# Even and odd layers of a three-layer transformer kernel: a moved transpose, two late weight parts, earlier query copies, and scalings shared with GpSimd

## The chip, the cores and the metric

The kernel runs on one core of a Trainium2 chip. A core has five engines that each run a program of their own: TensorE (PE in the profile; its weight loads are shown apart as PEld), VectorE (DVE), ScalarE (ACT), GpSimd (POOL) and SyncE (SP), which here only issues DMAs. The engines meet in semaphores: one instruction raises a semaphore when it ends, and another engine's program stands until the semaphore has the value it waits for. The metric is the device time of one execution in microseconds. The kernel before takes 1057.89 us, the median of three runs (1057.48 to 1059.09).

## What is computed

The program is a whole small model on 256 rows of 1024 columns: a first layer (attention, a recurrent block and a mixture of 32 experts), then two layers of another make, an even one and an odd one, each with a feed-forward block behind it, and a last norm. The change touches only the two later layers. Cut to what matters:

```python
# even layer: one product makes all inputs of two mixers
h = rmsnorm(x, norm_mix)
y = h @ ev_w_in        # qa_nope, qa_rope, c_kv, ka_rope, iq, ik, iw, qb, kb, vb
# dsa_mixer: attention over a latent
c_kv = rmsnorm(c_kv, kv_gain)              # "the latent rows", 128 columns
k_rope = rope(k_rope)
rel = relu(einsum(rope(iq), rope(ik)))     # picks keys for every query
idx = top_k(einsum(rel, iw), T // 4)
s = einsum([q_nope @ w_uk, rope(q_rope)], [c_kv, k_rope][idx])
o_a = (softmax(s) @ c_kv[idx]) @ w_uv
# diff_mixer: two softmaxes, one subtracted from the other
p = softmax(einsum(rope(qb), rope(kb)))    # 4 heads x 2 maps
o_b = rmsnorm((p[0] - lam * p[1]) @ vb)
x = x + concat(o_a, o_b) @ ev_w_out
x = x + swiglu(rmsnorm(x))

# odd layer: three attentions under one gate, 16 heads in 4 groups
y = rmsnorm(x) @ od_w_in   # qc, kc_raw, vc_raw, ks, vs, kw, vw, gates
g = sigmoid(gates)
o_cmp = softmax(rope(q) @ compress(rope(kc_raw))) @ compress(vc_raw)
o_slc = softmax(rope(q) @ rope(ks)[selected blocks]) @ vs
o_win = softmax(rope(q) @ rope(kw)[window]) @ vw
x = x + (g0 * o_cmp + g1 * o_slc + g2 * o_win) @ od_w_out
x = x + swiglu(rmsnorm(x))
```

With 256 rows the selected blocks and the window hold every earlier key, so both parts are plain causal attention, each over its own keys.

## The kernel before

**Products in two parts.** A product `h @ W` is made of f16 numbers: each factor is split into a high part (f16 of the number) and a low part (what is left), and three products are summed, high by high, low by high, high by low. ScalarE makes a weight tile's high part (`high_part`, L290), VectorE its low part (`low_part`, L297). The class `Projection` does this tile by tile over the columns of `W`, in two slots. `multiply` (L383) is one tile on TensorE: 48 matmuls, 16 for each of the three terms, and the weights' low part is only wanted from the 33rd on. Its argument `between` is called after each matmul and can put other work into the middle of a tile. `move` (L395) brings the result from PSUM to `y` on ScalarE. The next load into a slot waits for the low part of the tile before it there.

**Output weights.** The class `OutWeights` does the same for `ev_w_out` and `od_w_out`, in eight parts of 128 rows: `high_part` (L525) on ScalarE, `low_part` (L530) on VectorE, the semaphore `out.low` counting the latter.

**Even input product, `even_in`.** Twelve tiles (k = 0 to 11). Between the tiles stands the side work that needs columns already made. After tile 1 TensorE turns four blocks of `uk` and then the two blocks of the normalized latent rows (`turn`, L3256, waiting for `ckv_normed`); tile 2 follows; then the keys' product, which waits for ScalarE's copy of the turned latent rows (`ckv_out`, L3127). VectorE splits tiles and does one part of the rotary embedding (rope); GpSimd does another (L1487, L1488). Just before the end of tile 11 the keys are turned, which waits for both (`kb_begun`, `kb_ended`).

**Even attention, `even_attention`.** Eight units, four of `diff_mixer` (u = 0 to 3) and four of `dsa_mixer` (4 to 7). A unit is 2 x 256 rows of scores; because of causality each half is done in two row tiles, `SPAN`: tile 0 has 128 rows by 128 keys, tile 1 has 128 rows by 256 keys. TensorE scores a unit, VectorE finds the row minimum (the scores are negated), ScalarE takes exponentials and sums (L3367), VectorE weighs the unit (`weigh`: reciprocal of the sums, L3438, then scalings, L3442), TensorE turns it (L3534), VectorE and ScalarE copy it from PSUM (VectorE's is `left`, L3449), TensorE multiplies by the values (L3555), and ScalarE and VectorE split the result (`rest`, L3453). VectorE's loop runs ahead: in its step u it finds the minimum of unit u + 2, weighs unit u + 1 and copies unit u. The last two low parts of the output weights stand in this loop, after `left(4)` and `left(5)` (`LATE_LOWS`); TensorE waits for all eight (`out.low`) before its first projection, in unit 7.

**Odd input product, `odd_in`.** Ten tiles in the order of `ODD_TILES`. After tile 8 TensorE turns the doubled first keys (L3795), which waits for ScalarE's four copies of the turned queries (L3688, `q_out`) and its doubling of the keys (`keys_twice`); after tile 9 the second keys. At the start of step k ScalarE makes the high part of tile k + 1. VectorE's step k makes the low part of tile k + 1, a rope, and in step 5 the copies of the compressed keys (`c_out`).

**Odd attention, `sparse_attention`.** Sixteen units, two (selected blocks, window) for each of eight pairs of heads. A unit goes the same way as in the even attention. `weigh` multiplies the sums by the gate, takes the reciprocal (L3947) and scales four blocks (L3951). `turn` (L4036) makes six transposes of 128x128, three for each of the two heads: one of tile 0 and two of tile 1.

GpSimd has no part in the odd attention. Each engine's order is written by hand, as the order of these calls in its function.

## Time and profile before

| | before |
|---|---|
| median of three runs | 1057.89 us (1057.48 to 1059.09) |
| profiled execution, its own time | 1059.21 us |
| span of its records | 1057.2 us, 20482 instructions |
| mean granted clock of TensorE | 0.976 of full speed |
| TensorE busy | 967.5 us, 92% |
| VectorE busy | 592.9 us, 56% |
| ScalarE busy | 479.6 us, 45% |
| GpSimd busy | 103.3 us, 10% |
| chain that ended last | TensorE 65%, DMA 13%, VectorE 7%, ScalarE 4% |

The profile is one execution of the program. A row of the timeline has the start in us from the beginning of the span, the duration, the engine, the line of the kernel, the operation, output `<-` input, shapes and count; in brackets stands how long the engine was idle just before, and what ended that. A count above 1 means that several like instructions that follow each other are shown as one row, whose duration runs over all of them. A row of the table of stretches has for each engine the time that it was busy within the stretch, the granted clock of TensorE as a share of full speed, the share of the DMA engines' time and the rate in GB/s. "later_pB" is the PSUM of the later layers, and "field" the large SBUF area in which most of their buffers lie.

The even input product lies at about 425 to 497 us of the span, the even attention to 530, the feed-forward block behind it to 737, the odd input product to 797, the odd attention to 850.

### The profile page before, as it was taken

To read this page: it belongs to the slowest core of one execution; us is meant where nothing else is said; L and a number is where in the kernel's file an instruction comes from. 1 tells how busy PE (TensorE), PEld (TensorE's weight loads), DVE (VectorE), ACT (ScalarE), POOL (GpSimd) and SP (SyncE) were. 2 spreads that over 40 slices of the span, in tenths; PEclk is the share of its full clock that TensorE was granted. 3 is DMA by queue.
4 is the path that set the end of the run, shared out by engine and by line. 5 is a ranking of instruction groups with operands and counts; after the bars stand their busy time and mean duration, and the time that the engine had idled before them with its cause. 6 is when DMAs were issued, how large, how long until landed. Compare 5 with 4: busy or idle time off the path is not lost.

```text
span 1057.2 us, 20482 instructions
## 1 busy us (share of the span) xinstructions
PE 967.5 (92%) x8706; PEld 694.5 (66%) x8706; DVE 592.9 (56%) x965; ACT 479.6 (45%) x822; POOL 103.3 (10%) x110
## 2 busy tenths in 40 slices
PE   6999999989666678999999999999999999999996
PEld 5676896654333344887658777786986558777774
DVE  5577888611000004799766555554888856644643
ACT  5567653410000005665664535436656755553442
POOL 5620550000000001014010000000030000000000
PEclk9999999999888899999999999999999999999998
DMA  9755119899999997765044665673725023757621
GB/s 259 231 156 176 42 42 386 332 411 420 421 421 421 421 414 238 258 219 182 19 165 159 201 220 172 203 234 125 240 88 160 2 103 132 244 179 238 210 69 40
DMA packets 108747, 228.68 MB, mean 216 GB/s; under 512 B 7305, under 2 KB 86203, under 8 KB 94075
## 3 DMA queue, kind: packets, MB, share of 16 engines
q1 hardware_dynamic: 105691, 219.38, 57.7%
q0 software_dynamic: 2976, 8.14, 2.6%
q8 instruction: 60, 0.98, 0.4%
q14 instruction: 20, 0.16, 0.0%
HBM read 224.63 MB, written 1.05 MB: 213 GB/s over the span
## 4 chain that ended last, share of the span: by engine, by line
PE 65%; DMA 13%; DVE 7%; ACT 4%; SPq 2%; issue 2%; DVEq 0%; ACTq 0%
PE later_pB L923 20%; PE later_pB L932 10%; PE later_pB L383 6%; PE later_pB L879 4%; DMA ring<-in_w_down 4%; PE rw_pB L1403 3%; DMA ring<-in_w_up 3%; DMA mix<-in_w_gate 3%; DMA ring<-in_w_gate 3%; PE later_pB L911 2%; SPq L1271 2%; PE rw_pB L2474 1%; PE rw_pB L1424 1%; PE rw_pB L1432 1%; PE later_pB L4036 1%
## 5 line engine op out<-in xcount | busy, mean ns | idle before, releaser
L923 PE MATMUL later_pB<-field 128*128 128x256 f16 x1920 | 212.9, 273 | 0.0
L923 PEld LDWEIGHTS later_pB<-field 128*128 128x128 f16 x1920 | 187.8, 98 | 25.5
L752 DVE SCALAR_TENSOR_TENSOR field<-field 128x2048 f16<-128x2048 f32 x84 | 153.8, 1869 | 57.1 <-ACT field L647 57.1
L647 ACT ACTIVATE field<-field 128x2048 f16<-128x2048 f32 x84 | 126.4, 1567 | 15.8 <-DMA field<-in_ffn_w_up 9.6
L932 PE MATMUL later_pB<-field 128*128 128x512 f16 x528 | 117.7, 379 | 0.6 <-DVE field L752 0.6
L383 PE MATMUL later_pB<-field 128*128 128x256 f16 (+2 forms) x960 | 114.7, 274 | 0.6
L383 PEld LDWEIGHTS later_pB<-field 128*128 128x128 f16 x960 | 94.2, 99 | 13.5 <-ACT field L319 1.8
L1403 PE MATMUL rw_pB<-ring,kept 128*32 128x256 f32 x864 | 69.0, 415 | 25.7 <-DMA ring<-in_w_up 22.7
L932 PEld LDWEIGHTS later_pB<-field 128*128 128x128 f16 x528 | 51.5, 98 | 58.9 <-issue 1.5
L1335 DVE TENSOR_TENSOR rw_mu_a<-rw_pB,rw_mu_a 128x256 f32<-128x256 f32 x8 | 3.4, 424 | 122.9 <-PE rw_pB L1403 122.9
L1403 PEld LDWEIGHTS rw_pB<-ring,kept 128*32 128x32 f32 x864 | 37.9, 120 | 50.6 <-issue 37.1
L768 DVE SCALAR_TENSOR_TENSOR field<-later_pB,field 128x512 f32<-128x512 f32 x22 | 15.2, 691 | 91.6 <-ACT field L665 91.6
L665 ACT ACTIVATE field<-later_pB 128x512 f32<-128x512 f32 x22 | 13.1, 597 | 102.6 <-PE later_pB L923 102.5
L297 DVE SCALAR_TENSOR_TENSOR field<-wt,field 128x2048 f16<-128x2048 f32 (+2 forms) x22 | 52.7, 2397 | 12.2 <-ACT field L290 11.7
L290 ACT ACTIVATE field<-wt 128x2048 f16<-128x2048 f32 (+2 forms) x22 | 42.1, 1916 | 7.9 <-DMA wt<-in_od_w_in 4.3
L1424 PE MATMUL rw_pB<-ring,rw_mu_a 128*32 128x512 f32 x216 | 34.1, 668 | 11.3 <-DMA ring<-in_w_down 7.1
L879 PE MATMUL later_pB<-field 128*128 128x512 f16 x192 | 43.3, 380 | 0.0
L1294 ACT ACTIVATE rw_mu_a<-rw_pB 128x256 f32<-128x256 f32 x8 | 3.1, 388 | 77.9 <-PE rw_pB L1461 77.9
L1432 PE MATMUL rw_pB<-rw_few_y,rw_mu_a 128*128 128x512 f32 x64 | 29.8, 606 | 7.4 <-ACT rw_few_y L1303 6.5
L383 PE MATMUL in_pY<-ring 128*128 128x256 f16 (+1 forms) x288 | 33.8, 269 | 2.4 <-DVE ring L297 1.9
L665 ACT ACT_TABLE_LOAD x8 | 10.3, 1283 | 56.0 <-PE later_pB L923 44.6
L879 PEld LDWEIGHTS later_pB<-field 128*128 128x128 f16 x192 | 18.5, 98 | 21.9 <-issue 1.1
(589 smaller groups left out, 1563.6 us busy)
## 6 DMA issues: line engine op xcount, KB each, us to landing
ring<-in_w_up SPq DMA_DIRECT2D x27, 1024.0 KB, 26.7
ring<-in_w_gate SPq DMA_DIRECT2D x27, 1024.0 KB, 26.4
ring<-in_w_down SPq DMA_DIRECT2D x24, 1024.0 KB, 26.1
field<-in_ffn_w_down SPq DMA_DIRECT2D x22, 1024.0 KB, 5.0
field<-in_ffn_w_gate SPq DMA_DIRECT2D x20, 1024.0 KB, 7.5
field<-in_ffn_w_up SPq DMA_DIRECT2D x20, 1024.0 KB, 9.8
wt<-in_ev_w_in SPq DMA_DIRECT2D x9, 1024.0 KB, 5.8
wt<-in_od_w_in SPq DMA_DIRECT2D x9, 1024.0 KB, 5.5
```

The source lines that it names most:

```text
L290: self.nc.scalar.activation(self.w_hi[:, k % 2, :, 0:n], self.wt[:, k % 2, :, 0:n], ACT.Copy, scale=W_SCALE).then_inc(self.hi_ready, 1)
L297: self.nc.vector.scalar_tensor_tensor(self.w_lo[:, k % 2, :, 0:n], self.wt[:, k % 2, :, 0:n], W_SCALE, self.w_hi[:, k % 2, :, 0:n], ALU.mu ...
L383: ins = self.nc.tensor.matmul(self.pY[:, slot, t, 0:n], x[:, c, t * P:(t + 1) * P], w[:, slot, c, 0:n], start=(term == 0 and c == 0), stop ...
L647: copy = lambda o, i, scale=1.0: nc.scalar.activation(o, i, ACT.Copy, scale=scale)
L665: nc.scalar.activation(gated[:, s, :], pG[:, s, :], ACT.Silu, scale=1.0 / W_SCALE).then_inc(silu_done, 1)
L752: return nc.vector.scalar_tensor_tensor(out, whole, scale, hi, ALU.mult, ALU.subtract)
L879: return nc.tensor.matmul(pY[:, t, half_of(n)], source[:, c, t * P:(t + 1) * P], by[:, c, half_of(n)], start=(c == 0 and term == 0), stop= ...
L923: ins = T.matmul(p[:, s, j * SEQ:(j + 1) * SEQ], w[:, s, m, c, j::NJ], h[:, c, :], start=(n == 0), stop=(n == 3 * KC - 1))
L932: return T.matmul(pY[:, t, half_of(half)], h[:, s, at:at + P], w[:, s, j, half_of(half)], start=False, stop=stop, skip_group_check=True)
L1403: ins = nc.tensor.matmul(into[i * CAP:(i + 1) * CAP, 0:D_EXPERT], h[:, c, i * CAP:(i + 1) * CAP], held[:, c * D_EXPERT:(c + 1) * D_EXPERT] ...
L1424: ins = nc.tensor.matmul(pD[i * CAP:(i + 1) * CAP, half, :], hidT[:, j, i * CAP:(i + 1) * CAP], held[:, at:at + 512], start=(j == 0), stop ...
L1432: ins = nc.tensor.matmul(pY[:, t, half, :], into_tokens[:, g, t * P:(t + 1) * P], y[:, half * 512:(half + 1) * 512], start=(g == 0), stop= ...
```

## The change

Four edits, independent of each other.

**The latent turn.** `even_in` on TensorE: the wait for `ckv_normed` and the two transposes of the latent rows go from behind tile 1's side work into tile 2, after its first 14 matmuls (`between` is called from the ninth on, and `turn_latent` acts at its count 5).

```diff
+        def turn_latent(done):
+            if done == 5:
+                pe.wait_ge(ckv_normed, 1)
+                turn(half(0, 0), lambda t: ckv[:, t, :]).then_inc(ckv_turned, 1)
...
-            pr.multiply(pe, k, turn_keys if k == n_tiles - 1 else None)
+            pr.multiply(pe, k, {2: turn_latent, n_tiles - 1: turn_keys}.get(k))
             if k == 1:
                 pe.wait_ge(rows_in, 5 * 16)
                 pe.wait_ge(pr.low_T, KC)
                 for n in range(4):
                     nc.tensor.transpose(sc[:, 1, n * P:(n + 1) * P], uk[:, n, :], ident)
-                pe.wait_ge(ckv_normed, 1)
-                turn(half(0, 0), lambda t: ckv[:, t, :]).then_inc(ckv_turned, 1)
```

TensorE's order around tile 2 of the even input product, before; the row with two transposes of L3256 is the latent turn, the 96 matmuls are tiles 0 and 1:

```order
L363 MATMUL later_pB<-con_identity,mix 128x128 x16
L383 MATMUL later_pB<-field 128x248 x96
L3276 MATMUL later_pB<-con_identity,field 128x128 x4
L3256 MATMUL later_pB<-con_identity,field 128x128 x2
L383 MATMUL later_pB<-field 128x248 x48
L3282 MATMUL later_pB<-field 128x256 x4
L383 MATMUL later_pB<-field 128x256 x48
```

And after:

```order
L363 MATMUL later_pB<-con_identity,mix 128x128 x16
L383 MATMUL later_pB<-field 128x248 x96
L3281 MATMUL later_pB<-con_identity,field 128x128 x4
L383 MATMUL later_pB<-field 128x248 x14
L3256 MATMUL later_pB<-con_identity,field 128x128 x2
L383 MATMUL later_pB<-field 128x248 x34
L3285 MATMUL later_pB<-field 128x256 x4
```

The two transposes moved behind 14 of tile 2's 48 matmuls; nothing else on TensorE moved there.

**Late low parts.** `even_attention` on VectorE: the low parts 6 and 7 of the output weights leave steps 4 and 5 of the unit loop and come after the loop, ahead of `rest(6)`. On TensorE the wait for all eight parts becomes a wait in each projection, for 6 parts in the first six and for 7 and 8 in the last two.

```diff
-EVEN_LOWS, LATE_LOWS = {1: (0, 1), 2: (2,), 3: (3,), 4: (4,), 5: (5,)}, {4: 6, 5: 7}
+EVEN_LOWS, LATE_LOWS = {1: (0, 1), 2: (2,), 3: (3,), 4: (4,), 5: (5,)}, (6, 7)
...
-            if u in LATE_LOWS:
-                out.low_part(dve, LATE_LOWS[u])
...
             if u >= 6:
                 rest(u - 2)
+        for c in LATE_LOWS:
+            out.low_part(dve, c)
         rest(units - 2)
...
         def project(c):
             pe.wait_ge(low_out, min(c, units // 2) + 1)
+            pe.wait_ge(out.low, max(c + 1, LATE_LOWS[0]))
             project_first(c)
...
             if u == 7:
-                pe.wait_ge(out.low, KC)
                 project(0)
```

VectorE's order in steps 4 and 5 of the even attention before, from `left(4)` on; L530 is a low part of the output weights, L3438 the reciprocal at the head of a weighing:

```order
L3449 COPY field<-later_pB 128x384
L530 SCALAR_TENSOR_TENSOR field<-field 128x1024
L3438 RECIPROCAL ea_part<-ea_den 128x4
L3442 TENSOR_SCALAR field<-field,ea_part 128x128
L3442 TENSOR_SCALAR field<-field,ea_part 128x256
L3442 TENSOR_SCALAR field<-field,ea_part 128x128
L3442 TENSOR_SCALAR field<-field,ea_part 128x256
L3422 TENSOR_REDUCE ea_low_max<-later_pB 128x2 x2
L3449 COPY field<-later_pB 128x384
L530 SCALAR_TENSOR_TENSOR field<-field 128x1024
L3438 RECIPROCAL ea_part<-ea_den 128x4
```

VectorE's order at the end of the even attention after the change, from the last unit's copy on (L3456 is `rest`, L3493 the scaled outputs):

```order
L3456 TENSOR_TENSOR field<-later_pB,field 128x256
L3452 COPY field<-later_pB 128x384
L3456 TENSOR_TENSOR field<-later_pB,field 128x256
L530 SCALAR_TENSOR_TENSOR field<-field 128x1024 x2
L3456 TENSOR_TENSOR field<-later_pB,field 128x256
L3493 SCALAR_TENSOR_TENSOR field<-field,later_pB 128x1024
L3456 TENSOR_TENSOR field<-later_pB,field 128x256
```

Both low parts left the two steps, where a copy is now followed at once by the next reciprocal, and stand together ahead of the third remainder from the end.

**Query copies first.** `odd_in` on ScalarE: the high part of the last tile (9) goes from the start of step 8 to behind the query copies and the doubled keys. On VectorE the copies of the compressed keys go from step 5 to step 6, behind the low part of tile 7 and ahead of the rope of step 6.

```diff
-            if 1 <= k < n_tiles - 1:
+            if 1 <= k < n_tiles - 2:
                 pr.high_part(act, k + 1)
...
                 ins.then_inc(q_out, 1)
-            if k == 8:
                 act.wait_ge(x_turned, 1)
                 act.wait_ge(ks_roped, 1)
                 double(0, 1536).then_inc(keys_twice, 1)
+                pr.high_part(act, 9)
...
-            if 3 <= k <= 6:
-                dve.wait_ge(pr.moved, k)
-                rope(link, nc.vector, part(256 * (k - 3)), r64, tmp)
-            if k == 5:
+            if k == 6:
                 dve.wait_ge(seconds, 1)
                 dve.wait_ge(glink, 3)
...
                 nc.vector.tensor_tensor(o.vc[:], each, own, ALU.mult).then_inc(c_out, 1)
+            if 3 <= k <= 6:
+                dve.wait_ge(pr.moved, k)
+                rope(link, nc.vector, part(256 * (k - 3)), r64, tmp)
```

ScalarE's order in steps 8 and 9 of the odd input product before; L395 moves a tile's result, L290 is the last tile's high part, L3688 the copies of the queries (x4) and the doubled keys (x2):

```order
L395 ACTIVATE field<-later_pB 128x2x256
L290 ACTIVATE field<-wt 128x2432
L3688 ACTIVATE field<-later_pB 128x512 x4
L3688 ACTIVATE field<-field 128x512 x2
L395 ACTIVATE field<-later_pB 128x2x256
L3688 ACTIVATE field<-field 128x512 x2
```

And after:

```order
L395 ACTIVATE field<-later_pB 128x2x256
L3691 ACTIVATE field<-later_pB 128x512 x4
L3691 ACTIVATE field<-field 128x512 x2
L290 ACTIVATE field<-wt 128x2432
L395 ACTIVATE field<-later_pB 128x2x256
L3691 ACTIVATE field<-field 128x512 x2
```

The high part moved behind six copies; the count of instructions is the same.

**GpSimd scales tile 0.** `sparse_attention` gets a program for GpSimd: for every unit it waits for VectorE's reciprocal (`inverted`), scales the two blocks of tile 0 (2 x 128x128, L3942 of the new kernel), and raises `weighed_first`. VectorE scales only the two blocks of tile 1 (2 x 128x256); before it writes the factors of unit u it waits until GpSimd is done with unit u - 2. TensorE turns the four blocks of tile 1 first, then waits for `weighed_first` and turns the two of tile 0.

```diff
+    def gpsimd(pool):
+        t, c0, nk = SPAN[0]
+        wait_alone(pool, begun, cleared, 3)
+        for u in range(units):
+            at = u % 2
+            pool.wait_ge(inverted, u + 1)
+            for i in range(2):
+                into = E[:, at, i, c0:c0 + nk]
+                ins = nc.gpsimd.tensor_scalar(into, into, part[:, at, i, t:t + 1], None, ALU.mult)
+            ins.then_inc(weighed_first, 1)
...
+            if u >= 2:
+                dve.wait_ge(weighed_first, u - 1)
             link(nc.vector.tensor_tensor(part[:, at], den[:, at], gate[:, b + 1, 2 * n:2 * n + 2, :],
                                          ALU.mult))
-            link(nc.vector.reciprocal(part[:, at], part[:, at]))
+            nc.vector.reciprocal(part[:, at], part[:, at]).then_inc(inverted, 1)
+            dve.wait_ge(inverted, u + 1)
+            t, c0, nk = SPAN[1]
             for i in range(2):
-                for t, c0, nk in SPAN:
-                    into = E[:, at, i, c0:c0 + nk]
-                    ins = nc.vector.tensor_scalar(into, into, part[:, at, i, t:t + 1], None, ALU.mult)
+                into = E[:, at, i, c0:c0 + nk]
+                ins = nc.vector.tensor_scalar(into, into, part[:, at, i, t:t + 1], None, ALU.mult)
             ins.then_inc(weighed, 1)
...
-            for i in range(2):
-                for k, (t, kb, at) in enumerate(blocks):
+            for k, (t, kb, at) in sorted(enumerate(blocks), key=lambda b: -b[1][0]):
+                if t == 0:
+                    pe.wait_ge(weighed_first, u + 1)
+                for i in range(2):
                     ins = nc.tensor.transpose(pT[:, i, k * P:(k + 1) * P], E[:, u % 2, i, at:at + P], ident)
```

VectorE's order for one unit of the odd attention before; L3937 is a row minimum, L3945 and L3947 make the factors, L3951 scales, the copy is `left`:

```order
L3937 TENSOR_REDUCE nsa_low_max<-later_pB 128x2 x2
L3945 TENSOR_TENSOR nsa_part<-nsa_den,field 128x4
L3947 RECIPROCAL nsa_part<-nsa_part 128x4
L3951 TENSOR_SCALAR field<-field,nsa_part 128x128
L3951 TENSOR_SCALAR field<-field,nsa_part 128x256
L3951 TENSOR_SCALAR field<-field,nsa_part 128x128
L3951 TENSOR_SCALAR field<-field,nsa_part 128x256
L3958 COPY field<-later_pB 128x384
```

And after:

```order
L3953 TENSOR_REDUCE nsa_low_max<-later_pB 128x2 x2
L3963 TENSOR_TENSOR nsa_part<-nsa_den,field 128x4
L3965 RECIPROCAL nsa_part<-nsa_part 128x4
L3970 TENSOR_SCALAR field<-field,nsa_part 128x256 x2
L3977 COPY field<-later_pB 128x384
```

Of four scalings two are left on VectorE, and 32 scalings of 128x128 (16 units, two each) stand on GpSimd, which had none there.

## Rows read from the trace of the kernel before

**Rows 1.** table of stretches, the odd attention

```profile
797.00:850.00 53.00, 47.82 (x410) 31.27 (x409) 47.45 (x153) 37.20 (x152) 0.00 (x0) 1.00 0.20 64
```

**Rows 2.** timeline of the even input product, around the latent rows

```profile
429.98 0.44 PE L3256 MATMUL later_pB<-con_identity,field 128*128 128x128 f32 x2 [1.12 <-DVE field L3217]
...
430.25 5.24 PE L383 MATMUL later_pB<-field 128*128 128x248 f16 x48
...
433.83 0.59 ACT L3127 ACTIVATE field<-later_pB 128x512 f32<-128x512 f32 x1
```

**Rows 3.** timeline of the even attention, units 3 to 7

```profile
516.11 1.22 DVE L530 SCALAR_TENSOR_TENSOR field<-field 128x1024 f16<-128x1024 f32 x1
...
516.25 0.22 ACT L3367 ACTIVATION_READ_ACCUMULATOR field<-later_pB,ea_low_max 128x1 f32 x1
...
517.24 0.17 DVE L3438 RECIPROCAL ea_part<-ea_den 128x4 f32<-128x4 f32 x1
...
519.95 0.85 PE L3534 MATMUL later_pB<-con_identity,field 128*128 128x128 f32 x6 [1.32 <-DVE field L3449]
...
521.17 0.18 DVE L3438 RECIPROCAL ea_part<-ea_den 128x4 f32<-128x4 f32 x1 [0.19 <-ACT field L3367]
...
522.51 1.55 PE L3555 MATMUL later_pB<-field 128*64 128x256 f32 x8
...
527.76 0.87 PE L3555 MATMUL later_pB<-field 128*64 128x256 f32 x8
...
529.09 0.42 DVE L3453 TENSOR_TENSOR field<-later_pB,field 128x256 f16<-128x256 f32 x1 [2.30 <-ACT field L3387]
```

**Rows 4.** timeline of the odd input product, last two tiles

```profile
781.01 5.40 PE L383 MATMUL later_pB<-field 128*128 128x256 f16 x48
...
782.24 2.23 ACT L290 ACTIVATE field<-wt 128x2432 f16<-128x2432 f32 x1 [2.17 <-DMA wt<-in_od_w_in]
...
784.38 2.04 ACT L3688 ACTIVATE field<-later_pB 128x512 f32<-128x512 f32 x4
...
787.60 1.06 PE L3795 MATMUL later_pB<-con_identity,field 128*128 128x128 f32 x8 [1.18 <-ACT field L3688]
...
788.50 6.36 PE L383 MATMUL later_pB<-field 128*128 128x304 f16 x48
...
791.87 1.15 ACT L3688 ACTIVATE field<-field 128x512 f32<-128x512 f32 x2 [3.92 <-POOLq L3685]
```

**Rows 5.** timeline of the odd attention, turn of one unit on TensorE

```profile
826.18 0.85 PE L4036 MATMUL later_pB<-con_identity,field 128*128 128x128 f32 x6 [0.47 <-issue]
```

**Rows 6.** timeline of the even input product, tile splits and ropes on GpSimd

```profile
449.83 2.28 DVE L297 SCALAR_TENSOR_TENSOR field<-wt,field 128x2048 f16<-128x2048 f32 x1
...
471.75 1.32 POOL L1488 TENSOR_TENSOR field<-field,con_rope 128x512 f32<-128x512 f32 x1
...
472.16 3.07 DVE L297 SCALAR_TENSOR_TENSOR field<-wt,field 128x2048 f16<-128x2048 f32 x1 [0.20 <-ACT field L290]
...
485.07 0.73 POOL L1487 TENSOR_TENSOR field<-field,con_rope 128x256 f32<-128x256 f32 x1 [2.71 <-DVEq L3245]
```

**Rows 7.** timeline: scalings of one odd unit, and the nearest GpSimd instructions

```profile
22.14 2.80 POOL L1671 TENSOR_SCALAR fi_base<-ring 1x1024 f16<-1x1024 f32 x1 [6.49 <-DMA ring<-in_w_uq]
...
63.18 0.67 POOL L1684 CAST low<-con_diagonal 128x128 bf16<-128x128 f32 x1
...
535.67 0.23 POOL L3674 MEMSET field<- 128x128 f32 x1
...
827.33 1.01 DVE L3951 TENSOR_SCALAR field<-field,nsa_part 128x128 f32<-128x128 f32 x4
```

**Rows 8.** timeline of the first layer, GpSimd beside VectorE

```profile
130.10 2.25 POOL L2178 TENSOR_TENSOR rw_mu_a<-kept,rw_few_y 128x512 f32<-128x512 f32 x1
...
131.25 1.12 DVE L2895 TENSOR_SCALAR rw_mla_st<-rw_mla_st 128x2 f32<-128x2 f32 x1
```

**Rows 9.** table of stretches, one microsecond of the even attention

```profile
523.00:524.00 1.00, 1.00 (x9) 0.48 (x5) 0.62 (x3) 0.31 (x2) 0.00 (x0) 0.50 0.00 0
```

More of the change, by code:

```diff
@@ L3851 @@
 NSA_NAMES = ["scored", "least", "exped", "weighed", "probs_turned", "probs_left", "probs_right", "summed", "high_out", "low_out",
-             "c_scored", "c_less", "c_exped", "c_weighed", "c_turned", "c_out", "gate_exps", "vlink", "begun"]
+             "c_scored", "c_less", "c_exped", "c_weighed", "c_turned", "c_out", "gate_exps", "vlink", "begun", "inverted",
+             "weighed_first"]
 def sparse_attention(nc, ctx, sems, con, y, o, low, outT, out, room, pB, made, cleared, project_first, start):
@@ L3878, in sparse_attention @@
     (scored, least, exped, weighed, probs_turned, probs_left, probs_right, summed,
-     high_out, low_out, c_scored, c_less, c_exped, c_weighed, c_turned, c_out, gate_exps, vlink, begun) = sems
+     high_out, low_out, c_scored, c_less, c_exped, c_weighed, c_turned, c_out, gate_exps, vlink, begun, inverted,
+     weighed_first) = sems
     tiles_split, moved, q_out, ks_out, kw_out, kw_roped = made
@@ L4112, in tensor @@
             project(c)
-    return Engines(sync, scalar, vector, tensor)
+    return Engines(sync, scalar, vector, tensor), gpsimd
 AHEAD = {"in2": 248, "in3": 304}
@@ L4275, in last_layer @@
                     made = (pr_odd.lo_ready, pr_odd.moved, *(odd_side[n] for n in ("q_out", "ks_out", "kw_out", "kw_roped")))
-                    last["nsa"] = sparse_attention(nc, ctx2, nsa_sems, con, y_odd, o, low, oT, odd_weights, nsa_room, pB, made, cleared,
+                    last["nsa"], last["nsa_pool"] = sparse_attention(nc, ctx2, nsa_sems, con, y_odd, o, low, oT, odd_weights, nsa_room, pB, made, cleared,
                                                    project_first, start=block_loads("out3", 1))
@@ L4308, in _ @@
                         last_layer()
+                        last["nsa_pool"](pool)
                     @block.sync
```

## Prediction

> **What bounds the kernel now.** I read the table of stretches first [rows 1]: in the odd layer's attention, the emptiest of the four places that the change touches, TensorE is still busy in 47.82 of 53 us, and VectorE is as full (47.45). So a gain can only come out of the short waits of TensorE, and the second view is the timeline around each place that the change touches, with what ended the wait in brackets. Four such waits matter: 1.12 us for the latent rows [rows 2], 1.32 us for a copy by VectorE in the even attention [rows 3], 1.18 us for copies by ScalarE before the odd layer's last product [rows 4], and about 0.5 us in every second unit of the odd attention [rows 5]. Between them and behind them TensorE runs without a gap, in the feed-forward stretches above all, and what is won at one place reaches the end unless something else is late before the next.
>
> **Latent turn, -0.8 us.** Before, the two transposes start at 429.98, when VectorE has scaled the latent rows, and the 48 matmuls of tile 2 follow [rows 2]. Now 14 of these go first. 48 take 5.24 us, so 14 take 1.5 us; the wait began at 429.98 - 1.12 = 428.86, they end at 430.4, and the rows are there just ahead of 429.98. The wait of 1.12 us is gone; no instruction is added. Late next is the key product, which needs ScalarE's copies ending at 433.83 + 0.59 = 434.42, against 430.25 + 5.24 = 435.49 before: 1.05 is left. Tiles 3 to 11 have their parts in time, since ScalarE and VectorE do not follow TensorE here. But the stage ends on the turned keys, and these wait for GpSimd's second rope, which starts at 485.07 after VectorE has done its half of the keys [rows 6]. That chain moves only if VectorE moves, and VectorE has had no gap since 472.16. There its split of tile 9 took 3.07 us where the split at 449.83 took 2.28, with GpSimd's rope step of 471.75 to 473.07 beside it. That rope starts on the moved tile 7, so with TensorE 1.05 earlier the step ends at 472.0, before VectorE is ready: 0.79 comes back and goes down the chain to the turned keys. Bounds: nothing, if GpSimd's next step gets in front instead, and 1.12; I take 0.8.
>
> **Late low parts, -0.7 us.** The first (516.11, 1.22 us) stands ahead of the sixth weighing and so ahead of the copy that TensorE waits 1.32 us for [rows 3]. Without it the weighing waits for the exponentials, which end at 516.25 + 0.22 = 516.47. It started at 517.24: 0.72 of the 1.22 comes back, and TensorE's wait shrinks from 1.32 to 0.60. The second one wins nothing: the weighing behind it, at 521.17, waited for its exponentials. Both now come after the units: 2 x 1.22 = 2.44 us into a VectorE gap of 2.30 us that ends at 529.09 [rows 3]. The 0.14 us over is paid by the remainder at 529.09 and the scaled outputs behind it, and these are due only when the last unit's values are summed, which is TensorE's pace. The waits for parts 7 and 8 stand now before the last two of eight projections, some 8 us after the parts are made: nothing. Bounds 0 and 1.32.
>
> **Query copies first, -1.2 us.** TensorE stood 1.18 us at 787.60 for ScalarE [rows 4]: the 2.23 us split of the last tile, which had waited for its weights until 782.24, stood ahead of the four query copies (2.04) and the doubled keys. Now the copies start when the queries are turned, as tile 8 begins, say 781.2; the doubled keys, as long as the 1.15 at 791.87, end at 781.2 + 2.04 + 1.15 = 784.4 and the split at 786.6. TensorE leaves tile 8 at 781.01 + 5.40 = 786.4, so its transposes wait for nothing, and they cover the split: tile 9 is due at 787.4. The whole 1.18 goes. Moved with it: the tile's low part on VectorE comes about 2 us later, and tile 9 wants it after 32 of 48 matmuls, at 787.4 + 32/48 x 6.36 = 791.6; by the 3.07 of rows 6, for 256 columns against 304, the low part takes at most 3.7, so from 786.6 it is ready at 790.3. The window keys are doubled at 791.87 + 1.15 = 793.0 and TensorE, 1.18 earlier than 788.50 + 6.36, comes at 793.7: 0.7 us of cover, and without it the gain would be 0.5. The compressed keys' copies move behind the low part of tile 7; that part is 1.1 us earlier and the last tile's weights with it, but nobody waits for them any more: 0. Bounds -0.5 and -1.2.
>
> **GpSimd scales tile 0, 0 us.** VectorE's four scalings of a unit, two of 128 and two of 256 columns, take 1.01 us together [rows 7]. The two larger ones stay: between half (0.5) and two thirds (0.67) of it, I take 0.61, or 0.40 per unit less, if VectorE were alone. GpSimd scales two 128x128 blocks. No row shows that; a 128x128 cast took it 0.67, a multiplication by a number of 1024 columns 2.80, and a fill of 128 columns 0.23 [rows 7]. The 2.80 gives 0.35 for 128 columns; with a start of some 0.15 out of the fill's 0.23 that makes 0.5, which I take, with 0.23 and 0.67 as bounds. The two engines get in each other's way. A VectorE scaling of two columns took 1.12 us, more than the four large ones together, and ended at 132.37 with GpSimd's instruction, at 130.10 + 2.25 = 132.35 [rows 8]; in rows 6 VectorE paid 0.79. Here the first VectorE scaling goes at once, GpSimd starts a signal later and then holds the second one: the first takes 0.3, the hold 0.5 less the 0.1 by which it overlaps, the second 0.3: 1.0, the same as before. GpSimd's second block ends some 0.7 + 2 x 0.5 = 1.7 us after the reciprocal; the transposes of tile 1 go first, four of the six that take 0.85 [rows 5], and need VectorE's copy behind the scalings, of 0.5, so tile 0 is wanted at 1.0 + 0.5 + 0.6 = 2.1. So 0. Bounds: about eight weighings decide (two of the opening, one in each of four pairs of units, where TensorE's wait of 0.47 [rows 5] caps it, two at the end), so -0.40 x 8 = -3.2 if VectorE is not held; and with a block of p us, 12 x (p - 0.5) above it, since a longer weighing binds in nearly every unit: +2.0 at 0.67.
>
> The rule of the Trainium skill that bears on it is in "SBUF — State Buffer", § Who interferes with whom: a VectorE instruction in a mode with both ports, which a scaling can enter, and a GpSimd instruction exclude each other for the whole instruction, whoever comes first. Rows 8 agree (1.12 us for two columns). By that rule the term is 0, without it -3.2. Against it, "GPSIMD Engine Reference", § 4.1 Engine selection, calls GpSimd about as fast as line rate with one input; the cast of 0.67 us does not show that, and at a block of 0.25 us, an estimate from that page, the term would be about -2.
>
> **The sum.** -0.8 - 0.7 - 1.2 + 0 = -2.7. The profiled execution took 1059.21 us (span 1057.2, 2.0 around it) and would take 1056.5; it lay 1.3 over the median of the runs, 1057.89, from which I subtract: 1055.2. What a measurement can tell here from no change is about 0.2%, 2.1 us.
>
> **Rivals.**
> VectorE is not held. If its second scaling gets in before GpSimd, or the block is short, the fourth term becomes -3.2: 1052.0. For it: the second scaling follows the first within 0.3 us, and GpSimd has a signal to wait for and a start of its own. Against: rows 8. Chance 0.20.
>
> The clock stays up. After TensorE's wait of 1.32 us its granted clock was 0.50, the lower level (1.2 GHz), in the row of 523 [rows 9], and the eight value matmuls took 1.55 us where the next unit's took 0.87 [rows 3]; with the six transposes and six projections behind them that is some 1.5 us. A wait of 0.6 may leave it up: 1053.7. Against: sixteen one-column matmuls stand there too and stay. Chance 0.14.
>
> Gains lost at the joins. If GpSimd's rope gets in front (first term 0) and the exponentials or the window keys come later than I read, half of the 2.7 is left: 1056.7. For it: two of the terms hang on chains of VectorE and GpSimd that are full. Chance 0.20.
>
> GpSimd is slow, on the other side. If a block with a factor per row takes 1.0 us rather than 0.5, VectorE's weighing grows by 0.5 and GpSimd's second block misses the transposes: 12 x 0.5 = +6.0, and 1061.2. The gains are used up at p = 0.73, and it is slower by over 0.2% from 0.90. For it: no row has such a factor, and a GpSimd instruction of rows 8 took 2.25 us, held by VectorE in its turn. Against: the 128x128 cast of rows 7. Chance 0.10.
>
> **Numbers.** My forecast has 0.36 and a range of its own from 1054.2 to 1056.6. The range of all reaches from the first rival, 1051.8, to 1057.8, where the slow GpSimd begins. Faster: two thirds of the forecast, the first two rivals and a little of the third, 0.62. Slower: most of the last, 0.08. The rest, 0.30, is within 0.2%.
>
> **What would show it.** The transposes of the latent rows between two pieces of tile 2 without a wait; GpSimd's second rope starting near 484.3; the sixth weighing at 516.5 less the first gain, with TensorE's wait behind it near 0.6, and the clock after it; the transposes before the last odd tile without a wait; GpSimd blocks near 0.5 us and VectorE's second scaling of a unit drawn out; opening to last unit of the odd attention as long as before. It is wrong if the odd attention moves by over 1 us, or if the turned keys of the even layer come no earlier.

## The result and the profile after

The changed kernel takes 1051.08 us (median of six runs, 1048.93 to 1053.35) against 1057.68 (six runs, 1055.98 to 1059.36). The ratio is 0.9942, with a 95% interval of 0.9927 to 0.9956: 6.1 us less, between 4.6 and 7.7. The forecast was 2.7 less, and the time lies below its range. The profiled execution took 1053.35 us, 5.86 less than the one before.

The head of the page after; the second row has busy time, share and instructions of each engine:

```profile
span 1051.4 us, 20505 instructions
PE 969.4 (92%) x8706; PEld 693.2 (66%) x8706; DVE 587.2 (56%) x933; ACT 479.5 (46%) x822; POOL 123.2 (12%) x142
```

TensorE is busy 1.9 us more (969.4 against 967.5), which comes from the first layer, where its granted clock was lower in this execution (0.93 against 0.96 from 200 to 300 us); GpSimd works 20 us more, VectorE 5.7 less. So waits went. Where they went is read by dividing the span at four instructions that both kernels have: the start of the transposes of `uk` (428.26 before, 429.11 after; the first layer, which the change does not touch, took 0.85 longer in this execution), the first scores of the even attention, the start of its last value matmuls, the first scores of the odd attention, and the start of its last value matmuls.

| stretch, us | before | after | difference | forecast |
|---|---|---|---|---|
| `uk` transposes to first even scores | 65.88 | 65.16 | -0.72 | -0.8 |
| even attention, to its last values | 35.82 | 33.52 | -2.30 | -0.7 |
| feed-forward and odd input product | 265.62 | 264.24 | -1.38 | -1.2 |
| odd attention, to its last values | 60.54 | 58.34 | -2.20 | 0 |

The sum is -6.6, and with the 0.85 of the first layer -5.75, which is the difference of the two executions to about 0.1. Two stretches come out near their forecast and two do not. The table of stretches shows both attentions, first of before (even, odd), then of after; columns as in [rows 1]:

```profile
494.14:529.96 35.82, 34.00 (x242) 21.36 (x242) 27.33 (x83) 23.47 (x85) 0.00 (x0) 0.95 0.29 92
795.58:856.12 60.54, 55.36 (x463) 34.99 (x460) 50.56 (x160) 39.17 (x155) 0.00 (x0) 1.00 0.20 65
```

```profile
494.27:527.79 33.52, 32.42 (x243) 20.36 (x243) 27.36 (x83) 23.43 (x85) 0.00 (x0) 1.00 0.31 99
792.03:850.37 58.34, 55.43 (x462) 35.00 (x459) 46.46 (x128) 39.09 (x156) 22.28 (x32) 1.00 0.23 73
```

In the even attention the granted clock is 1.00 where it was 0.95, and TensorE is busy 1.58 us less for the same matmuls; the other 0.72 are idle time. In the odd attention TensorE is busy as long as before, and 2.27 us of idle time are gone; VectorE is busy 4.1 us less.

The timeline of the changed kernel, at the places of [rows 2 to 7]:

```profile
431.02 0.38 PE L3256 MATMUL later_pB<-con_identity,field 128*128 128x128 f32 x2
...
492.00 1.09 PE L3256 MATMUL later_pB<-con_identity,field 128*128 128x128 f32 x8 [0.30 <-POOLq L3124]
...
516.63 0.18 DVE L3441 RECIPROCAL ea_part<-ea_den 128x4 f32<-128x4 f32 x1 [0.31 <-ACT field L3370]
...
519.35 0.85 PE L3537 MATMUL later_pB<-con_identity,field 128*128 128x128 f32 x6 [0.59 <-DVE field L3452]
...
521.81 0.87 PE L3558 MATMUL later_pB<-field 128*64 128x256 f32 x8
...
524.66 2.35 DVE L530 SCALAR_TENSOR_TENSOR field<-field 128x1024 f16<-128x1024 f32 x2
...
782.01 2.25 ACT L290 ACTIVATE field<-wt 128x2432 f16<-128x2432 f32 x1
...
784.08 1.04 PE L3798 MATMUL later_pB<-con_identity,field 128*128 128x128 f32 x8
...
820.12 0.73 DVE L3970 TENSOR_SCALAR field<-field,nsa_part 128x256 f32<-128x256 f32 x2
820.18 1.39 POOL L3942 TENSOR_SCALAR field<-field,nsa_part 128x128 f32<-128x128 f32 x2 [2.14 <-DVE nsa_part L3965]
...
821.42 0.85 PE L4057 MATMUL later_pB<-con_identity,field 128*128 128x128 f32 x6 [0.20 <-issue]
```

The latent turn and the transposes ahead of the last odd tile have no bracket: TensorE does not wait there any more. The wait before the turn of unit 6 is 0.59, where [rows 3] had 1.32, and the eight value matmuls behind it take 0.87, where they took 1.55. In the odd attention VectorE's two scalings take 0.73 us where four took 1.01 [rows 7], although GpSimd's two, 1.39 us long, begin 0.06 us behind the first of them.

The same by form, line by line within 797 to 850 us, of before and then of after (busy us and mean ns behind the bar):

```profile
L3951 DVE TENSOR_SCALAR field<-field,nsa_part 128x256 f32<-128x256 f32 x30 | 10.4, 347 | 0.0
L3951 DVE TENSOR_SCALAR field<-field,nsa_part 128x128 f32<-128x128 f32 x31 | 8.8, 284 | 0.6
```

```profile
L3970 DVE TENSOR_SCALAR field<-field,nsa_part 128x256 f32<-128x256 f32 x31 | 11.4, 409 | 0.5
...
L3942 POOL TENSOR_SCALAR field<-field,nsa_part 128x128 f32<-128x128 f32 x32 | 22.3, 705 | 33.8 <-DVE nsa_part L3965 33.8
```

A GpSimd block takes 0.705 us in the mean (0.81 for a unit's first, beside VectorE's scalings, and 0.60 for its second), and a VectorE scaling of 256 columns 409 ns instead of 347: beside GpSimd it loses 0.06 us in the mean, not half a GpSimd instruction.

### The profile page after: what moved, and what is told of

Same layout as the page of the kernel before. It is cut to its first block, busy times and chain, and to the rows that moved or that the text cites. A ratio compares the mean times of both kernels' runs of the same rounds, so it can differ in the third digit from the quotient of the medians.

```text
span 1051.4 us, 20505 instructions
## 1 busy us (share of the span) xinstructions
PE 969.4 (92%) x8706; PEld 693.2 (66%) x8706; DVE 587.2 (56%) x933; ACT 479.5 (46%) x822; POOL 123.2 (12%) x142
## 4 chain that ended last, share of the span: by engine, by line
PE 64%; DMA 10%; DVE 10%; ACT 3%; SPq 3%; issue 1%; POOL 0%; DVEq 0%
PE later_pB L923 20%; PE later_pB L932 10%; PE later_pB L879 4%; DMA ring<-in_w_down 4%; PE later_pB L383 4%; PE rw_pB L1403 3%; DMA ring<-in_w_up 3%; DMA ring<-in_w_gate 3%; DVE field L297 2%; SPq L1271 2%; PE later_pB L911 2%; PE rw_pB L1424 2%; PE rw_pB L2474 1%; DMA wt<-in_ev_w_in 1%; PE rw_pB L1432 1%
## 5 line engine op out<-in xcount | busy, mean ns | idle before, releaser
L923 PEld LDWEIGHTS later_pB<-field 128*128 128x128 f16 x1920 | 187.8, 98 | 25.5
L383 PEld LDWEIGHTS later_pB<-field 128*128 128x128 f16 x960 | 94.2, 98 | 13.5 <-ACT field L319 1.8
L932 PEld LDWEIGHTS later_pB<-field 128*128 128x128 f16 x528 | 51.5, 98 | 58.9 <-issue 1.5
L1424 PE MATMUL rw_pB<-ring,rw_mu_a 128*32 128x512 f32 x216 | 37.5, 737 | 11.9 <-DMA ring<-in_w_down 8.0
L290 ACT ACTIVATE field<-wt 128x2048 f16<-128x2048 f32 (+2 forms) x22 | 42.1, 1917 | 7.7 <-DMA wt<-in_ev_w_in 5.6
L383 PEld LDWEIGHTS in_pY<-ring 128*128 128x128 f16 x288 | 27.1, 98 | 10.0 <-ACT ring L290 2.3
```

Of the source, the lines that this page charges most:

```text
L290: self.nc.scalar.activation(self.w_hi[:, k % 2, :, 0:n], self.wt[:, k % 2, :, 0:n], ACT.Copy, scale=W_SCALE).then_inc(self.hi_ready, 1)
L383: ins = self.nc.tensor.matmul(self.pY[:, slot, t, 0:n], x[:, c, t * P:(t + 1) * P], w[:, slot, c, 0:n], start=(term == 0 and c == 0), stop ...
L923: ins = T.matmul(p[:, s, j * SEQ:(j + 1) * SEQ], w[:, s, m, c, j::NJ], h[:, c, :], start=(n == 0), stop=(n == 3 * KC - 1))
L932: return T.matmul(pY[:, t, half_of(half)], h[:, s, at:at + P], w[:, s, j, half_of(half)], start=False, stop=stop, skip_group_check=True)
L1424: ins = nc.tensor.matmul(pD[i * CAP:(i + 1) * CAP, half, :], hidT[:, j, i * CAP:(i + 1) * CAP], held[:, at:at + 512], start=(j == 0), stop ...
```

## The experiments

Two theories went in. The prediction's: GpSimd's block holds VectorE's second scaling, and the late low parts win only the wait. The one from comparing the traces: VectorE is hardly held, so that the shorter weighing counts, and the clock stays up in the even attention.

**Each part alone.** The kernel before with one or two of the four edits, each as the diff of the change has it; a line of each:

```diff
+        for c in LATE_LOWS:
+            out.low_part(dve, c)
```

```diff
+                ins = nc.gpsimd.tensor_scalar(into, into, part[:, at, i, t:t + 1], None, ALU.mult)
```

```diff
+            pr.multiply(pe, k, {2: turn_latent, n_tiles - 1: turn_keys}.get(k))
...
+                pr.high_part(act, 9)
```

> The kernel before with the late low parts alone. By the prediction's term VectorE's sixth weighing comes 0.7 us earlier and TensorE's clock falls all the same: -0.7 us. By the theory of the clock the wait of TensorE before the turn of unit 6 shrinks from 1.3 to 0.6 us and its clock then stays at full speed in the even attention, so the value matmuls of unit 5, the transposes and the first projection behind them run at full speed as well: -2.2 us.

> The kernel before with GpSimd's scalings alone. By the prediction's term (GpSimd's second block holds VectorE's second scaling): 0. By the theory that VectorE is hardly held: its two scalings take 0.73 us instead of the 1.01 of four, one of the two weighings of each pair of units decides, so 8 x 0.28 = -2.2 us, and the pair of units repeats every 6.25 us instead of 6.5.

> The kernel before with the latent turn and the query copies (and the compressed keys' copies) alone. Both theories: -0.7 for the turned keys of the even layer and -1.3 for the last tile of the odd product, -2.0 us together; TensorE's clock falls in the even attention as before.

| kernel | ratio to before | 95% interval | us | even input | even attention | odd attention |
|---|---|---|---|---|---|---|
| late low parts | 0.9977 | 0.9965 to 0.9988 | -2.4 | 65.87 | 33.52 | 60.55 |
| GpSimd scalings | 0.9964 | 0.9951 to 0.9976 | -3.8 | 65.65 | 35.88 | 58.25 |
| latent turn, query copies | 0.9985 | 0.9970 to 1.0001 | -1.6 | 65.27 | 34.25 | 60.54 |

Each stretch moves with its own part and with no other, but for the even attention of the third kernel. The late low parts alone take 2.3 us off the even attention, as the theory of the clock had it. By the stretches GpSimd's part is worth 58.25 - 60.54 = -2.3, and its timed interval (-5.2 to -2.5) holds no zero: the prediction's 0 is out. That interval does not hold -2.3 either; no run shows where the rest of the timed -3.8 comes from. The third kernel spoiled the simple form of the clock theory. Its wait is as long as before, and yet its clock stayed up; the first two rows are its timeline, the third its table of stretches:

```profile
515.53 0.85 PE L3537 MATMUL later_pB<-con_identity,field 128*128 128x128 f32 x6 [1.32 <-DVE field L3452]
...
518.00 0.87 PE L3558 MATMUL later_pB<-field 128*64 128x256 f32 x8
```

```profile
489.72:523.97 34.25, 32.42 (x242) 20.35 (x243) 27.36 (x83) 23.43 (x85) 0.00 (x0) 1.00 0.30 96
```

So 34.25 - 33.52 = 0.73 is the wait alone, and what the clock adds depends on the execution.

**The clock, over more executions.** The changed kernel with one low part back, and both kernels once more.

```diff
+            if u == 4:
+                out.low_part(dve, 6)
...
-        for c in LATE_LOWS:
-            out.low_part(dve, c)
+        out.low_part(dve, 7)
```

> The changed kernel with the first of the two low parts back in step 4, ahead of the sixth weighing; the second stays behind the units. Both theories: TensorE's wait before the turn of unit 6 is 1.3 us again instead of 0.6, and the even attention, from its first scores to the last unit's values, takes 34.2 us instead of 33.5 at full clock. If a wait of 1.3 us always brings the clock down, it takes 35.8 as in the kernel before; if the wait is only one condition (the third run had it with the clock up), 34.2.

> The kernel before once more, for the clock: its wait of 1.32 us before the turn of unit 6 is the same as in the first profile. If the wait decides, the clock falls in the even attention (35.8 us, first scores to last values); if it is a matter of the single execution, it may stay up (34.2).

> The changed kernel once more, for the clock and for the spread of the stages: even input product 65.2, even attention 33.5 with the clock up, odd attention 58.3 us.

The table of stretches over the even attention of each of the three:

```profile
491.73:527.61 35.88, 34.05 (x242) 21.19 (x242) 27.36 (x83) 23.44 (x85) 0.00 (x0) 0.95 0.29 91
```

```profile
492.80:530.28 37.48, 35.66 (x242) 22.23 (x242) 27.34 (x83) 23.43 (x85) 0.00 (x0) 0.91 0.28 88
```

```profile
493.06:526.58 33.52, 32.42 (x243) 20.35 (x243) 27.35 (x83) 23.47 (x85) 0.00 (x0) 1.00 0.31 98
```

With the wait of 1.32 us the clock fell to 0.50 in four of five executions (before twice, GpSimd alone, one part back; not in the third kernel above), and cost 1.6 us in three of them and 3.2 in one. With the wait of 0.59 it fell in two of eight (both in experiments below whose even attention is that of the changed kernel), and cost 1.57. The shorter wait does not rule the fall out. That it makes it rarer is likely but not shown by these counts: if both waits brought the fall equally often, thirteen executions would part so unequally about once in twelve. The timed runs speak for it: the late low parts alone won 1.3 to 3.7 us, more than the wait's 0.73. What decides within one kernel stays open. The other two stretches of the changed kernel took 65.51 and 58.37 this time, where 65.2 and 58.3 were expected.

**One low part in step 5.** The same edit, one step later.

```diff
+            if u == 5:
+                out.low_part(dve, 6)
```

> The changed kernel with one low part put in step 5 of the even attention, where the second one stood before; the other stays behind the units. By the prediction the part in step 5 costs nothing, since the weighing behind it waits for its exponentials: the even attention takes 33.5 us as in the changed kernel. Rival, each of the two cost 0.7: 34.2.

The even attention took 33.51: the part in step 5 costs nothing, as the prediction had it. With the first part back the wait was 1.32 again, so all of the 0.73 belongs to that one. (The even input product of this execution took 69.61 us, a stretch that the edit doesn't touch; more on it below.)

**What of GpSimd's part does it.** Three kernels take the changed one apart: GpSimd raises its semaphore without scaling (tile 0 stays unscaled); TensorE turns in the old order; VectorE does all four scalings, tile 1 first, and GpSimd none.

```diff
-            for i in range(2):
-                into = E[:, at, i, c0:c0 + nk]
-                ins = nc.gpsimd.tensor_scalar(into, into, part[:, at, i, t:t + 1], None, ALU.mult)
-            ins.then_inc(weighed_first, 1)
+            pool.sem_inc(weighed_first, 1)
```

> The changed kernel, in which GpSimd does not scale tile 0 (its part of the odd attention is left out, the semaphore is raised without work). VectorE's two scalings of a unit stand alone: 0.61 us instead of 0.73. If VectorE's chain sets the pace of the pairs of units, the odd attention loses another 8 x 0.12 = 1.0 us (58.3 to 57.4, first scores to last values); if TensorE's own work sets it by now, less than 0.3.

```diff
-            for k, (t, kb, at) in sorted(enumerate(blocks), key=lambda b: -b[1][0]):
-                if t == 0:
-                    pe.wait_ge(weighed_first, u + 1)
-                for i in range(2):
+            pe.wait_ge(weighed_first, u + 1)
+            for i in range(2):
+                for k, (t, kb, at) in enumerate(blocks):
```

> The changed kernel with TensorE's old order of the turn: it waits for GpSimd's two blocks before its first transpose, and goes head by head. GpSimd's blocks end 1.45 us behind the reciprocal, VectorE's 0.79. By the prediction's step (the transposes of tile 1 cover GpSimd's second block) the new order is needed: TensorE stands 0.2 to 0.7 us more in each pair, and the odd attention takes 1 to 4 us more than 58.3. Rival, GpSimd is done in time anyway: no change.

```diff
             ins.then_inc(weighed, 1)
+            t, c0, nk = SPAN[0]
+            for i in range(2):
+                into = E[:, at, i, c0:c0 + nk]
+                ins = nc.vector.tensor_scalar(into, into, part[:, at, i, t:t + 1], None, ALU.mult)
+            ins.then_inc(weighed_first, 1)
...
-                        last["nsa_pool"](pool)
```

> The changed kernel without GpSimd: VectorE scales tile 1 first, raises the semaphore, then tile 0, and TensorE turns tile 1 first. VectorE's load is that of the kernel before (1.01 us of scalings a unit). If the gain comes from VectorE's shorter weighing: 60.5 us as before, at most 0.5 less. If it comes from TensorE starting its turn earlier: 58.3.

The odd attention in the table of stretches, first without GpSimd's work, then with the old turn, then with VectorE doing all:

```profile
791.13:848.55 57.42, 55.20 (x463) 35.01 (x460) 44.77 (x128) 39.17 (x156) 0.00 (x0) 1.00 0.24 74
```

```profile
788.38:848.83 60.45, 55.31 (x462) 35.01 (x460) 46.50 (x128) 38.99 (x156) 22.27 (x32) 1.00 0.23 71
```

```profile
789.62:850.16 60.54, 55.30 (x463) 35.00 (x460) 50.60 (x160) 39.10 (x156) 0.00 (x0) 1.00 0.22 70
```

Without GpSimd's work VectorE's scalings take 350 ns each (mean of 32), and the odd attention loses another 0.92, where 8 x 0.12 = 1.0 was expected: VectorE's weighing still sets the pace, and eight weighings count. With the old order of the turn the whole gain is gone (60.45), since TensorE then waits for GpSimd, 0.62 us in this unit of its timeline:

```profile
825.64 0.85 PE L4056 MATMUL later_pB<-con_identity,field 128*128 128x128 f32 x6 [0.62 <-POOL field L3942]
```

And the new order without GpSimd gives nothing (60.54). Neither half is worth anything alone: GpSimd shortens VectorE's chain, and TensorE's order hides that GpSimd is slow.

**GpSimd's work twice.** Each block is first scaled into a spare buffer, then in place.

```diff
+                nc.gpsimd.tensor_scalar(spare[:, 2 * at + i, :], into, part[:, at, i, t:t + 1], None, ALU.mult)
                 ins = nc.gpsimd.tensor_scalar(into, into, part[:, at, i, t:t + 1], None, ALU.mult)
```

> The changed kernel, GpSimd doing each scaling twice (once into a spare buffer, once in place): four instructions a unit, its last block done some 2.85 us behind the reciprocal instead of 1.45. VectorE's two scalings stay at 0.73, since a GpSimd scaling hardly holds it. TensorE has about 0.2 to 0.6 us of cover for tile 0, so 0.8 to 1.2 us more in at least one unit of each pair: the odd attention takes 58.3 + 7 to 58.3 + 14 us. Should the cover be larger than the earlier runs show, less.

```profile
823.43 0.63 PE L4061 MATMUL later_pB<-con_identity,field 128*128 128x128 f32 x4
...
824.79 0.44 PE L4061 MATMUL later_pB<-con_identity,field 128*128 128x128 f32 x2 [0.74 <-POOL field L3946]
```

The odd attention took 65.61, +7.3 on the changed kernel, at the lower end of what was expected. The two transposes of tile 0 now stand apart from the four of tile 1 and wait for GpSimd. The cover is short: a GpSimd block twice as long turns the gain of 2.2 into a loss of 5.

**The two engines by themselves.** A small kernel with series of like instructions, on data of their own. Its series:

```python
v_scale = lambda i: v.tensor_scalar(t["va"][:, i * 256:i * 256 + 256], t["va"][:, i * 256:i * 256 + 256], t["vs"][:, 0:1], None, ALU.mult)
v_split = lambda i: v.scalar_tensor_tensor(t["vh"][:, i], t["vb"][:], 64.0, t["vg"][:], ALU.mult, ALU.subtract)
g_scale = lambda i: g.tensor_scalar(t["ga"][:, i * 512:i * 512 + 128], t["ga"][:, i * 512:i * 512 + 128], t["gs"][:, 0:1], None, ALU.mult)
g_product = lambda i: g.tensor_tensor(t["ga"][:, i * 512:i * 512 + 512], t["gb"][:], t["gc"][:], ALU.mult)
```

> A small kernel that computes nothing of the reference: it stores zeros, and VectorE and GpSimd run series of like instructions on their own data, alone and beside each other: VectorE's scaling of 128x256, its split of 128x2048 to f16, its scaling of 128x2; GpSimd's scaling of 128x128 and its product of two tensors of 128x512. If GpSimd's instruction holds VectorE for its whole length, VectorE's scaling beside GpSimd's scaling takes as long as GpSimd's (0.6 us and more) instead of some 0.35. If it is only some 0.1 us, the hold belongs to GpSimd's products of two tensors, and those draw out VectorE's scaling and split, while GpSimd's scaling does not.

Its groups by form, each taken within its own section (mean ns behind the comma). First VectorE's scaling of 256 columns alone, beside GpSimd's scalings, beside GpSimd's products; then its scaling of 2 columns alone and beside the products; then its split alone and beside the products; last GpSimd's scaling alone and beside the split:

```profile
L15 DVE TENSOR_SCALAR va<-va,vs 128x256 f32<-128x256 f32 x16 | 4.3, 349 | 0.0
...
L15 DVE TENSOR_SCALAR va<-va,vs 128x256 f32<-128x256 f32 x16 | 5.3, 408 | 4.8 <-POOL ga L18 4.8
...
L15 DVE TENSOR_SCALAR va<-va,vs 128x256 f32<-128x256 f32 x16 | 12.3, 845 | 10.1 <-POOL ga L19 10.1
...
L17 DVE TENSOR_SCALAR va<-va,vs 128x2 f32<-128x2 f32 x16 | 2.2, 222 | 1.2 <-POOLq L67 1.2
...
L17 DVE TENSOR_SCALAR va<-va,vs 128x2 f32<-128x2 f32 x16 | 10.9, 759 | 2.3 <-POOL ga L18 2.3
...
L16 DVE SCALAR_TENSOR_TENSOR vh<-vb,vg 128x2048 f16<-128x2048 f32 x8 | 17.7, 2286 | 0.1
...
L16 DVE SCALAR_TENSOR_TENSOR vh<-vb,vg 128x2048 f16<-128x2048 f32 x8 | 25.2, 3214 | 2.2 <-POOL ga L18 2.2
...
L18 POOL TENSOR_SCALAR ga<-ga,gs 128x128 f32<-128x128 f32 x8 | 4.7, 605 | 10.8 <-DVEq L50 10.8
...
L18 POOL TENSOR_SCALAR ga<-ga,gs 128x128 f32<-128x128 f32 x8 | 20.3, 2556 | 19.9 <-DVE vh L16 19.9
```

Two scalings side by side cost each other little: 349 to 408 ns, just what the changed kernel shows (409). Beside GpSimd's products of two tensors the means are 845 ns, and 759 for a scaling of 2 columns, but these means mix two kinds: eight of the sixteen scalings are held to the end of a product, 1.35 us each, and the others are free. One pair of each kind from the timeline, first beside a product, then beside a GpSimd scaling:

```profile
37.59 1.31 POOL L19 TENSOR_TENSOR ga<-gb,gc 128x512 f32<-128x512 f32 x1
37.70 1.35 DVE L15 TENSOR_SCALAR va<-va,vs 128x256 f32<-128x256 f32 x1
...
22.20 0.68 POOL L18 TENSOR_SCALAR ga<-ga,gs 128x128 f32<-128x128 f32 x1
22.28 0.45 DVE L15 TENSOR_SCALAR va<-va,vs 128x256 f32<-128x256 f32 x1
```

Beside the product the scaling ends behind it; beside GpSimd's scaling it loses 0.1 us and ends first. VectorE's split, which reads two tensors, holds GpSimd's scaling from 605 ns to 2556. So a product of GpSimd holds a scaling of VectorE for its whole length, and a scaling of GpSimd does not. Why is not shown: the product reads two tensors and is also four times as wide (512 columns against 128), and no run parts the two. Nor does a product hold whatever VectorE does. In the kernel before, VectorE's search for the eight largest (MAX8) took 0.29 us in the middle of a GpSimd product, and 0.29 again at 492.88, where GpSimd was idle:

```profile
476.44 1.28 POOL L1490 TENSOR_TENSOR field<-field,con_rope 128x512 f32<-128x512 f32 x1
476.84 0.29 DVE L3099 MAX8 field<-field 128x8 f32<-128x128 f32 x1
```

## Why the prediction was wrong, and where it was right

**GpSimd scales tile 0: the step that failed.** The prediction wrote that GpSimd "starts a signal later and then holds the second one", so that VectorE's weighing stays at 1.0. It took 0.73. The row behind that step [rows 8] is a VectorE scaling beside a GpSimd *product of two tensors*, and the 3.07 of [rows 6] likewise lies beside a product; the change adds GpSimd *scalings*. The small kernel reproduces the hold for products (349 ns to 1.35 us) and not for scalings (349 to 408). The first rival, that VectorE is not held, had the right outcome, though not for its reason: the second scaling does not get in before GpSimd, which starts 0.06 us behind the first. Its price was 0.40 x 8 = 3.2 and is 0.28 x 8 = 2.2, since 0.06 us of each scaling are lost after all. The count of eight weighings held.

The rule drawn on there, from the Trainium skill, "SBUF — State Buffer", § Who interferes with whom, is for a VectorE instruction in a mode with both ports. The scalings may well be in one, by the rows: 128 columns more lengthen a scaling by 63 ns (284 to 347) and a MAX8 by twice that (0.29 to 0.43 us, the latter at 491.89 in the kernel before). Beside products they agree with the rule (1.35 us, held to the end), beside GpSimd's scalings they do not (0.45 us, and done first). The same section of the Trainium skill says that a VectorE instruction with at most one input in SBUF, outside those modes, does not contend with GpSimd; MAX8 agrees (0.29 us with and without a product).

The size of GpSimd's block was wrong too, 0.705 instead of 0.5, and by the prediction's own bound ("+2.0 at 0.67") that should have cost over 2 us. It did not, because that bound let every longer block lengthen VectorE's weighing, which it does not. That the transposes of tile 1 cover GpSimd's second block was right, and more decisive than the prediction had it: without that order the gain is nil.

**Late low parts: the mechanism right, the size not.** The wait shrank from 1.32 to 0.59, the 0.7 that the prediction worked out, and the second part costs nothing in step 5. The other 1.57 of the profiled pair are the clock, priced at 1.5 as a rival with a chance of 0.14. The runs put this between: the fall comes in four of five executions with the long wait and in two of eight with the short one, so the mean gain, a rough estimate from these few counts, is about 0.73 + (4/5 - 2/8) x 1.6 = 1.6 us. The prediction counted the clock as all or nothing, and its row [rows 9] as fixed, though one profile can't tell a fixed cost from one that comes and goes.

**Query copies: right.** The stretch took 264.24 to 264.26 us in nine executions with it and 265.54 to 265.90 in four without: 1.4 less, against 1.2 forecast. The whole wait of 1.18 went and the split after the copies was in time; where the other 0.2 comes from is not shown.

**Latent turn: the size near, the way wrong, so luck.** -0.72 in the profiled pair, against -0.8. The prediction's step was that GpSimd's rope step would be over before VectorE's split of tile 9, whose 3.07 us [rows 6] would fall to 2.28. The rope did start earlier (41.03 us after the `uk` transposes, against 42.15), but then its next step lay beside the split, which took 3.12; for that case the prediction had written "nothing". What came back lies further on. Before, GpSimd's last step of this rope ran on beside VectorE's next split and held the first product of VectorE's half of the keys; after, it is over by then. The first two rows are of before, the others of after:

```profile
479.15 3.21 POOL L1492 TENSOR_TENSOR field<-field 128x512 f32<-128x512 f32 x1
481.14 1.50 DVE L1487 TENSOR_TENSOR field<-field,con_rope 128x256 f32<-128x256 f32 x1
...
473.31 3.12 DVE L297 SCALAR_TENSOR_TENSOR field<-wt,field 128x2048 f16<-128x2048 f32 x1 [0.15 <-DVE field L3199]
...
479.02 1.27 POOL L1492 TENSOR_TENSOR field<-field 128x512 f32<-128x512 f32 x1
...
482.36 0.41 DVE L1487 TENSOR_TENSOR field<-field,con_rope 128x256 f32<-128x256 f32 x1
```

The product starts 0.37 later, counted from the `uk` transposes, and takes 0.41 instead of 1.50: 0.72 less. It is 0.41 or 0.42 in all nine executions with the turn and 1.49 or 1.50 in the four without, and the split takes over 3.0 in all thirteen. TensorE now waits 0.30 for GpSimd's rope before the turned keys, the chain that the prediction named.

Over the executions: 65.15 to 65.61 in seven with the turn, 65.65 to 65.99 in four without, means 65.37 and 65.85, so -0.5. But two more with the turn took 66.90 and 69.61, and with them the mean of the nine is 66.0: over all of them nothing is shown to be won. In both, ScalarE's split of a late weight tile waited over 4 us for its DMA, and TensorE behind it nearly 2 us. The rows are of the kernel with GpSimd's work twice:

```profile
470.58 3.13 DVE L297 SCALAR_TENSOR_TENSOR field<-wt,field 128x2048 f16<-128x2048 f32 x1 [0.15 <-DVE field L3199]
...
480.74 1.91 ACT L290 ACTIVATE field<-wt 128x2048 f16<-128x2048 f32 x1 [4.28 <-DMA wt<-in_ev_w_in]
...
484.26 1.06 PE L3256 MATMUL later_pB<-con_identity,field 128*128 128x128 f32 x8 [1.88 <-ACT field L3127]
```

ScalarE waits for this load in all nine executions with the turn (1.30 to 4.37 us) and in none of the four without. The load is issued when VectorE's split of tile 9, in the same slot, ends (at 473.74 and 473.71 in the rows' kernel). In the two late executions GpSimd was already at the fourth step of its rope when that split began, not at the third, and the split began 1.5 and 2.4 us later than in the changed kernel's profile. The load itself then took 7.0 and 7.1 us instead of 5.4. So part of the delay hangs on the earlier rope, which the turn brings; why GpSimd got one step further in these two, and why the load took longer, no run tells.

**The sum.** With the means of the runs, -0.5 - 1.6 - 1.4 - 2.2 = -5.7, within the timed interval of -7.7 to -4.6; with the two executions of the late load counted, the first term is +0.2 and the sum -5.0, within it too. Of the 3 us beyond the forecast in the first sum, 2.2 are GpSimd's term and 0.9 the clock. The prediction had both as rivals, each by itself, and no sum for both together.

## What to carry to other kernels

When a row is taken as the price of contention, the row's own operation must match on both engines: here GpSimd's product of two tensors held VectorE's scaling, GpSimd's scaling did not, and MAX8 was not held by the product. A forecast that comes out needs its path read as well as its size: the latent turn won its 0.7 us at an instruction that the prediction did not name. Work given to a slower engine pays only if its consumer is reordered with it; the halves were worth nothing apart. A clock that falls behind a wait has to be counted over several executions before it is put into a sum.

## What the hardware showed beyond expectation

VectorE's split of 2048 columns and GpSimd's product of two tensors hold each other: 2286 to 3214 ns for the one, and in the same section 3304 ns for GpSimd's product, which took 1262 alone. The clock of the same kernel, at the same place and with the same wait, cost 1.6 us in one execution and 3.2 in another.
